# Residual, y and output rows of each tile issued by GpSimd between its gathers instead of by SyncE

## The reference

```python
x = x + mix @ w_out
ffn = peer_ffn(rmsnorm(x, norm_ffn).reshape(-1, D_MODEL), w_query, sub_keys, u_table, v_table)
x = x + ffn.reshape(x.shape)
# in peer_ffn, for 128 rows at a time:
q = (xc @ w_query).reshape(PEER_CHUNK, PEER_HEADS, 2, PEER_HALF)
s = jnp.einsum('thcd,hckd->thck', q, keys)
top_s, top_i = lax.top_k(s, PEER_TOPK)            # two halves, 16 each
best_s, best_j = lax.top_k(cand_s, PEER_TOPK)     # of the 256 sums
idx = jnp.take_along_axis(cand_i, best_j, axis=-1)
gate = jax.nn.softmax(best_s, axis=-1)
act = gelu(jnp.einsum('thkd,td->thk', u_table[idx], xc))
return jnp.einsum('thk,thkd->td', gate * act, v_table[idx])
```

## Time and profile before

| | us |
|---|---|
| median of 3 runs | 3236.37 |
| lowest and highest | 3235.67, 3245.21 |
| the profiled execution, time | 3233.63 |
| the profiled execution, span on the core | 3231.7 |
| DMA engines' packets, software queue (gathers) | 86.3% of 16 engines' span |
| DMA engines' packets, SP's queue | 5.6% |
| POOL busy | 1353.0 (42%) |
| DVE busy | 2137.6 (66%) |
| PE busy | 2272.4 (70%) |

### The profile page before, as it was taken

The page is one execution under the profiler, slowest core; times in us unless marked ns, Lnnn a source line. Parts: engine busy times, 40 slices in busy tenths (PEclk is TensorE's granted clock), DMA queues, the critical chain, the costliest instruction groups (busy, mean ns, idle before and its releaser), DMA issues.

```text
span 3231.7 us, 28466 instructions
## 1 busy us (share of the span) xinstructions
PE 2272.4 (70%) x7579; PEld 777.9 (24%) x7579; DVE 2137.6 (66%) x5164; ACT 942.7 (29%) x3204; POOL 1353.0 (42%) x1266
## 2 busy tenths in 40 slices
PE   8999877766776677566756675668566756685576
PEld 4556543311221122112211121112111211121121
DVE  4446577787578657865786568656865686568654
ACT  3223244323222322232223222322232223222222
POOL 1232034444444444444444444444444444444542
PEclk9999989978886888778878887878688978787899
DMA  5224589999999999999999999999999999999998
GB/s 198 80 76 96 206 337 387 374 388 401 418 421 418 418 410 421 412 420 417 420 407 417 418 421 408 413 413 420 412 422 416 421 405 417 417 421 411 420 421 334
DMA packets 187986, 1208.00 MB, mean 374 GB/s; under 512 B 26601, under 2 KB 34329, under 8 KB 47361
## 3 DMA queue, kind: packets, MB, share of 16 engines
q0 software_dynamic: 157344, 1142.99, 86.3%
q1 hardware_dynamic: 30480, 63.21, 5.6%
HBM read 1190.30 MB, written 15.42 MB: 373 GB/s over the span
## 4 chain that ended last, share of the span: by engine, by line
DMA 33%; PE 23%; DVE 16%; issue 7%; ACT 5%; POOL 4%; DVEq 0%; POOLq 0%; ACTq 0%
DMA uv_ring<-in_uv_table,idx 33%; PE ACC L2126 14%; DVE uv_ring L1922 9%; PE ZS L2046 6%; POOL uv_ring L1549 3%; ACT dg L1694 2%; PE ZS L2021 1%; ACT dot L1687 1%; ACT dot L1674 1%; DVE idx_f L1844 1%; PE ZS L2007 1%; DVE S L1843 1%; DVE pos L1767 1%; DVE pos L1764 0%; DVE best L1766 0%
## 5 line engine op out<-in xcount | busy, mean ns | idle before, releaser
L2126 PE MATMUL ACC<-uv_ring,dg 128*64 128x512 f32 x4352 | 1451.4, 778 | 911.1 <-ACT dg L1694 910.8
L1549 POOL DMA_INDIRECT uv_ring<-in_uv_table,idx x1088 | 1256.0, 1154 | 1530.4 <-PE ACC L2126 1302.4
L1922 DVE CUSTOM_DVE_ANT_0 uv_ring<-uv_ring,xn 128x1024 f32<-128x1024 f32 x1088 | 1327.5, 1226 | 728.2 <-DMA uv_ring<-in_uv_table,idx 693.4
L2126 PEld LDWEIGHTS ACC<-uv_ring,dg 128*64 128x64 f32 x4352 | 339.9, 165 | 1951.7 <-ACT dg L1694 1395.3
L1674 ACT ACTIVATE dot<-dot 128x2 f32<-128x2 f32 x544 | 110.6, 203 | 1879.3 <-DVE dot L1922 1879.2
L1694 ACT ACTIVATE dg<-stack,dot 128x64 f32<-128x64 f32 x1088 | 324.1, 340 | 17.7
L1687 ACT ACTIVATE dot<-gate,dot 128x1 f32<-128x1 f32 x1088 | 261.2, 287 | 18.9
L2046 PE MATMUL ZS<-score_w,xnT 128*128 128x512 f32 x512 | 242.9, 615 | 0.0
L518 PE MATMUL PJ<-w_in,xc 128*128 128x512 f32 (+1 forms) x384 | 141.0, 523 | 1.3 <-DVE pj L407 1.3
L2046 PEld LDWEIGHTS ZS<-score_w,xnT 128*128 128x128 f32 x512 | 93.3, 194 | 157.3 <-issue 157.3
L1922 DVE DVE_READ_ACCUMULATOR2_ANT dot<- 128x1 f32 x1088 | 88.8, 82 | 0.0
(11 more groups left out here) (353 smaller groups left out, 1590.5 us busy)
## 6 DMA issues: line engine op xcount, KB each, us to landing
uv_ring<-in_uv_table,idx POOLq DMA_INDIRECT x1088, 11.0
score_w<-in_w_query SPq DMA_DIRECT2D x8, 1024.0 KB, 19.1
w_in<-in_w_in SPq DMA_DIRECT2D x8, 640.0 KB, 9.3
xt<-in_x SPq DMA_DIRECT2D x9, 512.0 KB, 4.6
xr<-scratch_x SPq DMA_DIRECT2D x9, 512.0 KB, 8.3
xc<-in_x_columns SPq DMA_DIRECT2D x8, 512.0 KB, 3.7
out_y<-S SPq DMA_DIRECT2D x8, 512.0 KB, 7.7
scratch_u<-pj SPq DMA_DIRECT2D x9, 256.0 KB, 2.1
```

The costliest lines, as they stand in the source:

```text
L1549: pool.indirect_dma_start(out=ring[:, s_ % RING, :], out_offset=None, in_=a["uv_table"], in_offset=bass.IndirectOffsetOnAxis(ap=idx[:, s_: ...
L1922: V.tensor_tensor_reduce(row, row, xn[:, g, :], 1.0, 0.0, ALU.mult, ALU.add, dot[:, s_:s_ + 1]).then_inc(dots, 1)
L2126: ins = nc.tensor.matmul(ACCS[t % 2][GT * g:GT * (g + 1), b, :], dg[:, n % DG, :], ring[:, n % RING, D + 512 * b:D + 512 * b + 512], start ...
```

## The change

The three kinds of DMA become functions that take the engine, and POOL calls them inside its loop of gathers: `load_xr(t + 1)` behind the gather of slot 10, `out(t - 1)` behind that of slot 20, and `load_y(t + 2)` behind that of slot 28 (52 in the first turn). `load_xr(0)` and `load_y(1)`, which stood among SP's loads of weights at the start of the phase, are issued by POOL too. SP keeps the store of the 64 sample rows. The waits of each DMA are the same as before; the wait of `out` for its landing is gone from the issuer, and a landing now raises `out_stored` itself.

```diff
--- before.py
+++ after.py
@@ -1371,6 +1371,7 @@
         SPREAD = NSLOT - KS + 9
         SUM_AT, OUT_AT = LEAD + 1, LEAD + 5
         EARLY_Y = {"first": 106, "steady": 100}
+        XR_AT, STORE_AT, Y_AT = RING + 2, RING + OUT_AT + 4, {"first": 52, "steady": 28}
 
         BLOCKS = ((0, 1, 16), (1, 2, 8), (2, 4, 5), (4, 8, 3), (8, 16, 1))
         NCAND = sum((a1 - a0) * b for a0, a1, b in BLOCKS)
@@ -1428,12 +1429,12 @@
         keys_in, glu_in, b_glu_in, y_in = early.keys_in, early.glu_in, early.b_glu_in, early.y_in
         made, taken = c.sem("score_w_made"), c.sem("score_w_taken")
         g_ssm_in, bottom, xr_in = c.sem("g_ssm_in"), c.sem("weights_e2"), c.count("xr_in", 16)
-        stored = c.sem("stored_e")
         k = {n: c.count(n) for n in (
             "y_gelu y_turned yT_done z_done zb_done gate_y yn_done yn_turned ynT_done bot_done xr_done "
             "xn_done xn_turned xnT_done s_a s_b S_a S_b topped_a topped_b "
             "idx_ready idx_rest best_shifted ex_done gate_ready gate_rest xn_spread_a xn_spread_b xn_taken_a xn_taken_b acc_begun acc_taken "
-            "ss_o_done out_ready out_stored ms_y_done ms_x_done ms_o_done rs_y_done rs_x_done rs_o_done").split()}
+            "ss_o_done out_ready ms_y_done ms_x_done ms_o_done rs_y_done rs_x_done rs_o_done").split()}
+        k["out_stored"], samples_out = c.count("out_stored", 16), c.sem("samples_out")
         first = {n: c.sem(f"first_{n}") for n in "s S topped nmax ex idx gate".split()}
         wq_in = [c.sem(f"wq_in{e}") for e in range(EH)]
         uv_in = [c.sem(f"uv_in{i}") for i in range(RING)]
@@ -1445,6 +1446,21 @@
         def row_is_in(eng, t, s_):
 
             eng.wait_ge(uv_in[s_ % RING], t * (16 * NSLOT // RING) + 16 * (s_ // RING + 1))
+
+        def load_y(eng, t):
+
+            k["yn_turned"].held(eng, t - 1)
+            y_in.mark(eng.dma_start(y, s["y_ssm"][bass.ts(t, P), :]))
+
+        def load_xr(eng, t):
+
+            k["acc_begun"].held(eng, t - 1)
+            xr_in.mark(eng.dma_start(xr[:], s["x1"][bass.ts(t, P), :]))
+
+        def out(eng, t):
+
+            k["out_ready"].held(eng, t)
+            k["out_stored"].mark(eng.dma_start(a["y"][bass.ts(t, P), :], xo[:]))
 
         def slots_of(turn):
 
@@ -1492,10 +1508,6 @@
 
             @block.sync
             def _(sp):
-                def load_y(t):
-                    k["yn_turned"].held(sp, t - 1)
-                    y_in.mark(sp.dma_start(y, s["y_ssm"][bass.ts(t, P), :]))
-
                 def load_keys(n):
                     sp.wait_ge(made, QUARTERS * 2 * (n - 1))
                     sp.nop(nofuse=True)
@@ -1504,23 +1516,9 @@
                 def load_queries(e):
                     sp.dma_start(wq_rows[:, 2 * e:2 * e + 2], a["w_query"][e]).then_inc(wq_in[e], 16)
 
-                def load_xr(t):
-                    k["acc_begun"].held(sp, t - 1)
-                    xr_in.mark(sp.dma_start(xr[:], s["x1"][bass.ts(t, P), :]))
-
-                def out(t, n):
-                    k["out_ready"].held(sp, t)
-                    dst = a["y"][bass.ts(t, P), :] if n == P else a["y"][SEQ:SEQ + n, :]
-                    sp.dma_start(dst, xo[0:n, :]).then_inc(stored, 16)
-                    sp.wait_ge(stored, (t + 1) * 16)
-                    sp.nop(nofuse=True)
-                    sp.sem_inc(k["out_stored"].sem, 1)
-
-                k["out_stored"].prime(sp)
                 load_queries(0)
                 sp.dma_start(g_ssm[:], a["g_ssm"]).then_inc(g_ssm_in, 16)
                 sp.dma_start(w_bot[:], a["w_out"][AW:D, :].rearrange("(k p) n -> p k n", p=P)).then_inc(bottom, 16)
-                load_xr(0)
                 sp.dma_start(g_ffn[:], a["g_ffn"].to_broadcast([P, D])).then_inc(bottom, 16)
                 load_queries(1)
                 sp.dma_start(place[:].rearrange("p n k -> p (n k)"), a["place"].to_broadcast([P, 2 * KS])).then_inc(tables_in, 16)
@@ -1529,17 +1527,12 @@
                     load_queries(e)
                 sp.dma_start(stack[:], a["stack"]).then_inc(weights, 16)
                 sp.dma_start(g_fin[:], a["g_final"].to_broadcast([P, D])).then_inc(weights, 16)
-                sp.wait_ge(early.y_stored, 16 * 4)
-                load_y(1)
                 load_keys(2)
                 load_keys(3)
-                for t in range(PT - 1):
-                    load_xr(t + 1)
-                    load_y(t + 2)
-                    out(t, P)
-                load_xr(PT)
-                out(PT - 1, P)
-                out(PT, NS_ROWS)
+                k["out_ready"].held(sp, PT)
+                sp.dma_start(a["y"][SEQ:SEQ + NS_ROWS, :], xo[0:NS_ROWS, :]).then_inc(samples_out, 16)
+                k["out_stored"].held(sp, PT - 1)
+                sp.wait_ge(samples_out, 16)
 
             @block.gpsimd
             def _(pool):
@@ -1561,6 +1554,12 @@
                         elif turn != "first" and s_ == EARLY:
                             k["idx_rest"].held(pool, t)
                         gather(t, s_)
+                        if s_ == XR_AT and turn != "samples":
+                            load_xr(pool, t + 1)
+                        if s_ == STORE_AT and turn != "first":
+                            out(pool, t - 1)
+                        if turn in Y_AT and s_ == Y_AT[turn]:
+                            load_y(pool, t + 2)
                         if turn != "first" and s_ == RING + SUM_AT + 1:
                             root("o", t - 1, ms_o, rs_o)
                         if s_ >= RING:
@@ -1577,8 +1576,10 @@
 
                 for n in ("rs_y_done", "rs_x_done", "rs_o_done"):
                     k[n].prime(pool)
+                load_xr(pool, 0)
                 pool.wait_ge(early.y_stored, 16 * 4)
                 root("y", 0, ms_y, rs_y)
+                load_y(pool, 1)
                 root("x", 0, ms_x, rs_x)
                 retrieve("first", 0)
                 for t in range(1, PT - 1):
```

## The result

| | before | after |
|---|---|---|
| median (22 runs each), us | 3240.39 | 3247.26 |
| lowest and highest, us | 3232.08, 3246.08 | 3241.52, 3256.49 |
| ratio, 95% interval | | 1.0024 (1.0018 to 1.0030) |
| profiled execution: time and span, us | 3233.63, 3231.7 | 3245.91, 3244.1 |

The change costs 0.24%, 6.9 us. That is less than the 0.3% called "no change", and inside the range given (3219 to 3250), but it is no zero: the interval excludes one, and a second measurement of the same kernel gave 1.0025 (1.0016 to 1.0035). The forecast was a gain of 0.07%. The before of the forecast was also 4 us low: many runs have their median at 3240, and the execution whose trace was read was one of the fastest.

The account below looks back on a forecast made before the run. The prediction took the DMA engines' bytes as the bound. All terms were 0 except 2.5 us gained near slot 30: 3233.63 - 2.5 = 3231.1 us on the profiled execution, about 3234 us as median, range 3219 to 3250 us.

Parts of the forecast that it names:

- What bounds the kernel: Whole kernel: DMA engines wait for bytes at about 421 GB/s; only 4.0 us of a 325.9 us turn are anything else.
- The bytes stay: Per turn, the moved DMAs are 1.31 MB, 3.1 us, before and after; uniting the two queues gives 0 us.
- POOL's added work: POOL issues 25 more DMAs, 14 to 36 us of engine time, hidden by its waits for PE and the queue: 0 us.
- The waits that come onto POOL, and the landings: At slots 10, 20, 28 (52): no wait blocks POOL, and landings after 11 to 14 us are in time; 0 us.
- Where they fall: y behind slot 28 fills the hole at slot 30, gaining 2.5 us (0 to 3.7); stores and xr change 0 us.
- the term of 2.5 us: Gain from y's 0.62 us of bytes passing in idle DMA time near slot 30, in four turns.
- What would show it wrong: Signs: DMA rate falling behind each store, turns near 322 us, gathers idle on POOL's own issue, DVE waiting for xr.
- its bound, 36 us: Cost of POOL's added issues if the cover were gone at every one of the 25 DMAs; given no chance of its own.
- the queue of 5.5 us: Gathers on the DMA engines: one issued 1.4 us later still stands 5.5 us behind others, so the delay is hidden.
- the store that holds the gathers: Rival: each store on POOL's queue stops the next gather 2.3 us until its report; 18 us slower, 3254 us; chance 0.14.
- SP's transfers as what keeps the turn from its floor: Rival: SP's transfers at slots 8 to 14 cause at most half of each turn's 4.0 us loss; 3222 us; chance 0.17.

Follow-up runs that it names:

- The late places alone: All moved DMAs issued by SP instead of POOL, at the moments the changed kernel issues them (slots 10, 20, 28 or 52); 1.0004 against the kernel before.
- The no-operations: 24 no-operations more on POOL behind the gather of slot 60 of each turn but the first, added to the kernel after; 1.0021 against the kernel before.

## Why the prediction was wrong

The forecast was 0.07% less, and 0.24% more was measured.

- *What bounds the kernel*: right. The DMA engines' bytes; a loss of 1 us a turn in their feeding was seen in the time.
- *The bytes stay*: right as a sum. *POOL's added work*, "I take 0": right for the issues themselves, 0.6 us each, at the low end of the bounds, and the stores alone gave 1.0006. Wrong in what they set off: with them POOL's stall stands at a fixed slot, in front of a root (see the step that failed).
- *The waits that come onto POOL, and the landings*: right. But for the 1.8 us once ahead of y, no idle time stands ahead of the three in the turns, and the stores landed after 12.0 us, where 11 to 14 were forecast.
- *Where they fall*: the term of 2.5 us. The hole filled as forecast, even the stretch at 0 to 40 us with it, 1.5 us a turn instead of 0.4. But the time did not come. With the root at slot 11 the same turn loses 0.8 us at 110 to 230 and 0.5 us more at its end, and its sum is that of before. With y at slot 90 it is the largest hole that shrinks (2.0 to 2.7 us, now 1.3), the sum falls to 3.4 us, and the ratio is still 1.0003. The forecast took each hole as time lost. That a turn's holes are rather what remains between its bytes and the pace of DVE, ACT and PE, so that most of what is filled in one place opens in another, fits these sums but is argued: no run changed that pace.
- *The step that failed*: "The stores at slot 20 and xr at slot 10 fall in full stretches as before: 0 us." Only the new places were asked about. The old places, 36 to 46 us into a turn, lie right behind DVE's wait for the root, 2.7 us a turn, which stood in the trace of before and was not read. Those bytes kept the DMA engines busy while its lateness ran through the ring. Taken away, and with the root 1.8 us later, the engines run dry: 1.0 us a turn at 40 to 70 us. It takes both. The late places alone gave 1.0004, and the lateness comes from the plain DMAs on POOL, which tie its stall to the slot of the root; with the root ahead of the stall 7.2 of the 8.6 us went. The seven losses of 1.0 us come near the 6.9 us measured partly by luck: with the holes that closed and opened elsewhere, the turns of the profiles show 4 to 6 us more, and where the rest lies is open.
- *What would show it wrong*: "idle time of gathers put down to POOL's own issue" went up, from 208.4 us in before to 260.0 us in after, but the sum is no measure of the cost. It is 265.3 us with the root at slot 11 and 284.8 us with y at 90, which are not measurably slower than before. Some 36 us of it is one wait that the profile files under another name, in front of slot 122 of turns 1 to 6 (lines below). The mark was in where the stalls stand, 2.1 us in front of a root, not in how much they sum to. And I had given its bound, 36 us, no chance, since the queue of 5.5 us covers a late gather. It does; it doesn't cover a root that stands behind the late gather and that DVE needs now, once SP's transfers are gone from there.
- *The rivals*: the store that holds the gathers is refuted (1.0006, 1.0004 at slot 28). SP's transfers as what keeps the turn from its floor is refuted too (turns of 326.8 to 327.1 us, not near 322): moving them away gained nothing.

The gather of slot 122 in turn 4, before and after:

```profile
2056.83 0.94 POOL L1549 DMA_INDIRECT uv_ring<-in_uv_table,idx  x1 [5.75 <-PE ACC L2126]
```

```profile
2067.49 0.94 POOL L1542 DMA_INDIRECT uv_ring<-in_uv_table,idx  x1 [6.12 <-issue]
```

## What to carry to other kernels

Ask of a transfer that moves not only what it meets at its new place, but what it covered at the old one. On an in-order engine that issues DMAs, look at the small computing step behind an issue: a queue of gathers hides a late issue, but a late step that another engine waits for was hidden here only by other transfers that happened to lie there, so put it a place or two earlier as soon as its input is ready. And don't book a filled hole in the DMA rate as time gained: here 0.6 us of bytes moved into a hole changed no time that could be measured.

## What the hardware showed that was not expected

POOL's gathers stall by themselves. In before such a gap of 3.1 us from one gather to the next, where 1.2 to 1.7 us is usual for a pair, comes at every 106th gather, at the same slots in both profiles and in the other kernels without a plain DMA on POOL in the turns. With one plain DMA or more per turn on POOL one stands at a fixed slot in turns 2 to 7, 14 to 16 gathers ahead of the turn's last plain DMA: between slots 5 and 6 for the stores alone at 20, 13 and 14 for them at 28, 20 and 21 for all three with the store at 36; between 10 and 11, 12 and 13, 73 and 74 for y at 26, 28 and 90 with all three on POOL. The no-operations didn't shift it, and with y at 30 none was seen, though it could be hidden in front of slot 16.

Here DVE doesn't cause it: in the rows of turn 4 of after DVE is idle for 4.59 us, from 1783.60 us to 1788.19 us, and the 2.10 us of the stall, up to 1786.61 us, lie inside.

The Trainium skill's page "SBUF — State Buffer", in the box on the "DVE blocks DMA" trap, would have a two-port operation of DVE lock POOL out of writing descriptors; by that rule the 25 added issues were exposed. For them this trace doesn't agree: the longest took 0.65 us, and this stall has no DVE operation in it. Whether the rule is behind the gathers whose issue takes up to 2.0 us, in before and after alike, no run tested. What POOL does in these 2 us the profile doesn't show, and it stays open.
